# Half-height second product in the scores of the dilated attention

## The chip, the cores and the metric

The program runs on one NeuronCore of a Trainium2 chip. The metric is the device time of one execution in microseconds (us); of several executions the median counts. TensorE (PE in the profile) multiplies: it first loads a stationary operand of up to 128 rows by 128 columns (a weight load, PEld) and then streams a moving operand through it, one step per output column. The rows are the SBUF partitions over which a product sums. VectorE is DVE, ScalarE is ACT, GpSimd is POOL, SyncE is SP.

## The reference

Two transformer blocks stand one after the other, for 512 tokens of width 1024. The second one is a gated feed-forward layer, a mixing layer and another gated feed-forward layer. The change lies in the mixing layer's attention: twelve heads of width 64 in three groups of four, where group 0 looks back 128 tokens, group 1 looks back 512 tokens in steps of 4 and group 2 looks back 2048 in steps of 16. For every head

```
s = einsum('brnqhd,brnkhd->brnhqk', qb, kk) * (Dh ** -0.5)
s = where(allowed, s, -inf);  p = exp(s - max(s))
o = einsum('brnhqk,brnkhd->brnqhd', p, vv) / sum(p)
```

and the three groups' outputs are mixed by a softmax over their log denominators, which for head j is one softmax over the keys of all three groups together.

## The kernel before

Five programs, one for each engine, are written out in order; semaphore waits tie them together, and nothing is reordered by a scheduler. All matrix products work in parts: an operand x is split into a high part rounded to the type fp32r and a low part, the rest, and a product becomes high times high, low times high and high times low.

For the scores, a head has width 64 and the array has 128 rows, and the kernel uses this: `DQ` holds for a head (`key = 2 * g + e_half`) the high part of the queries in the head's own 64 rows and the low part in the other 64 rows. `DKH` holds the high part of the keys in both halves. One product over 128 rows of `DQ` with `DKH` is then (high + low) of the queries times high of the keys. `DKL` holds the low part of the keys in the head's own 64 rows only; the other 64 rows hold zeros, so that a second product over all 128 rows adds high of the queries times low of the keys.

The zeros are written by GpSimd in `pool_dilated` (six copies, one for each of the three groups and two halves), after its last piece of the normalised input and before it multiplies by the rotary cosines. TensorE waits for them (`misc_pool`, "zeros") in `pe_d_scores`.

`pe_d_scores(s)` is called for 16 steps s: j = s // 4 is the head in its group, i = s % 4 the block of 128 queries. It covers up to ten blocks of 128 keys, laid side by side in three PSUM banks (`SALL`), in runs of adjacent blocks of one group; each run is one pair of matmuls of one width. For i = 0 there are 3 runs (width 128 each), for i = 1 3 runs (256), for i = 2 4 runs (256, 256, 128, 384), for i = 3 5 runs (256): 60 runs in all over the 16 steps, 40 of width 256, 16 of 128 and 4 of 384.

There is one set of the three banks. So scores(s+1) wait until DVE has taken the masked maximum of scores(s) (`dve_d_max`, instructions of L86, which also move the scores to SBUF). ACT then takes the exponential, DVE divides by the sum (`dve_d_soft`, L79), TensorE transposes the result (`pe_d_turn`, L69, 128 wide), ACT and DVE copy it back, and TensorE multiplies it with the values (`pe_d_values`, stationary operand of 128 rows by 64 columns, shown as 128*64). On TensorE the loop over s is: scores(s+3), transposes(s), values(s-1). Scores 0 and 1 stand between parts of the projection v2, scores 2 before the loop. At s = 5 the projections of queries and keys for the second half of the heads are put in; then TensorE runs steps 5 to 12 without another large part. After values(7), DVE and ACT also write out the first half's result (`act_d_out`, `dve_d_out`). On DVE the loop is: maximum(s+3), copy(s), division(s+1).

Of the kernel before, what the change touches and what calls it, by code (L numbers as in the profile page):

```python
# [4 lines left out]
S = 512  # L5
# [141 lines left out]
def bass_two_blocks(nc, A, out):  # L147
    ctx = ExitStack()
    with ctx:
# [10 lines left out]
        def sb(shape, dt, offset):  # L160
            names[0] += 1
            return nc.alloc_sbuf_tensor_at(f"t{names[0]}", shape, dt, offset=offset)
# [43 lines left out]
        ZERO = RS[:, 9:10]  # L206
# [56 lines left out]
        DKL = sb([128, 6, S], F32R, AR + 24 * KB)  # L263
# [181 lines left out]
        def count(name):  # L445
            counts.append(Count(name))
            return counts[-1]
# [11 lines left out]
        hmul, h_hi, h_lo, h_lo_pool = count("h_scaled"), count("h_hi"), count("h_lo"), count("h_lo_pool")  # L459
# [8 lines left out]
        misc, misc_act, misc_pool = count("small_dve"), count("small_act"), count("small_pool")  # L468
# [501 lines left out]
        def pool_rotate(e, g, hf, cosv):  # L970
            tm = TMP[ta["rot", g, hf]][:, COLS[hf]]
            e.wait_ge(acc, ("rot", g, hf))
            e.tensor_tensor(tm, tm, cosv[:, COLS[hf]], ALU.mult).then_inc(by_cos, (g, hf))
# [12 lines left out]
        def rows_of(e_half):  # L986
            return slice(64 * e_half, 64 * e_half + 64), slice(64 - 64 * e_half, 128 - 64 * e_half)
# [1191 lines left out]
        def pool_glu_norm(e, nm):  # L2179
            pool_normed(e, nm, 0, UPPER)  # L2180
            pool_normed(e, nm, 1, ALL)
# [8 lines left out]
        def blocks(i):  # L2190
            out_ = [(0, kb) for kb in ((i - 1, i) if i else (0,))]
            return out_ + [(1, kb) for kb in range(i + 1)] + [(2, kb) for kb in range(i + 1)]
# [70 lines left out]
        def pe_d_scores(e, s):  # L2263
            j, i = s // 4, s % 4
            a, e_half = j // 2, j % 2
            runs = []
            for c, (g, kb) in enumerate(blocks(i)):
                if runs and runs[-1][1] == g and c % 4:
                    runs[-1][3] += 1
                else:  # L2270
                    runs.append([c, g, kb, 1])
            for b in range(3):
                banks.take(("ds", s, b), (maxes, ("dx", s)), at=b)
                e.wait_for(banks.free(("ds", s, b)))
            for c, g, kb, n in runs:
                key = 2 * g + e_half
                e.wait_ge(part_lo, ("dq", a, key))
                e.wait_ge(part_hi, (("dk", a, key), 1))
                e.wait_ge(part_lo, (("dk", a, key), 0))
                e.wait_ge(misc_pool, "zeros")  # L2280
                q, kh, kl = DQ[:, key, :], DKH[:, key, :], DKL[:, key, :]
                qs, ks = slice(128 * i, 128 * i + 128), slice(128 * kb, 128 * (kb + n))
                o = SALL[:, 128 * c:128 * (c + n)]
                e.matmul(o, q[:, qs], kh[:, ks], start=True, stop=False)
                t = e.matmul(o, q[:, qs], kl[:, ks], start=False, stop=True)
            t.then_inc(acc, ("ds", s))

        def dve_d_max(e, s):
# [128 lines left out]
        def pool_pz_pool(e, n):  # L2417
            tm = PZ_TMP[n]
            e.wait_ge(misc, ("window", n))
            e.wait_ge(cnt_in, "all")  # L2420
            e.wait_ge(acc, ("dv", 14 if n < 2 else 15))
            e.tensor_tensor(tm[:, :], PZ[:, (n + 1) % 2, 16:16 + S], CNT[:, n, :], ALU.mult).then_inc(
                misc_pool, ("mean", n))
            e.wait_ge(misc_pool, ("mean", n))
            e.tensor_tensor(tm[:, :], tm[:, :], PZC[n][:, :], ALU.subtract).then_inc(misc_pool, ("pool", n))
# [57 lines left out]
        def pe_dilated(e):  # L2483
# [5 lines left out]
            banks.only(3, 4, 5, 6, 7)  # L2489
            pe_linear(e, "v2", WX["v2"], [(0, 256)] * 4, h_tokens(n_mix), lambda n, hf: (v_done, ("dv2", n)), swap=True,  # L2490
                      mid={(F, 0, 0): lambda: pe_rotate(e, pending, F, rot), (F, 0, 2): lambda: pe_d_scores(e, 0),
                           (F, 0, 3): lambda: pe_d_scores(e, 1)})
            pe_d_scores(e, 2)
            for s in range(16):
                if s == 5:
# [170 lines left out]
        def pool_dilated(e):  # L2666
            pool_glu_norm(e, n_mix)
            e.wait_ge(acc, ((("w2", 1, 2), 1), 3, 1))
            e.dma_start(DCOS[:, :], A["k_dcos"]).then_inc(dil_in, by=16)
            e.dma_start(DSIN[:, :], A["k_dsin"]).then_inc(dil_in, by=16)  # L2670
            e.dma_start(rot, A["k_drot"]).then_inc(dil_in, by=16)
            e.dma_start(DM[:, :, :], A["k_dil"]).then_inc(dil_in, "all", by=16)
            e.wait_ge(h_lo_pool, ("mix", 7, 1))
            for s in range(6):
                _, other = rows_of(s % 2)
                if s:
                    e.wait_ge(misc_pool, ("zero", s - 1))
                e.tensor_copy(DKL[other, s, :], ZERO[other, :].to_broadcast([64, S])).then_inc(
                    misc_pool, ("zero", s), "zeros")
            e.wait_ge(misc_pool, "zeros")  # L2680
            e.wait_ge(dil_in, "all")
            for a in range(2):
                for kind in ("dk", "dq"):
                    for n in range(3):
                        pool_rotate(e, (kind, a, n), F, DCOS)
            e.wait_ge(acc, ("ds", 15))
            e.dma_start(CNT[:, :, :], A["k_cnt"].to_broadcast([128, 4, S])).then_inc(cnt_in, "all", by=16)
            for n in range(4):
                pool_pz_pool(e, n)
# [118 lines left out]
        def pool_program(e):  # L2808
            pool_begin(e)
            pool_mla_in(e)  # L2810
            pool_mla(e)
            pool_swa(e)
            pool_ff1(e)
            pool_glu_norm(e, n_glu1)
            pool_normed(e, n_mix, 0, LOWER)
            pool_dilated(e)
            pool_normed(e, n_glu2, 0, LOWER)
            pool_glu_norm(e, n_glu2)
# [109 lines left out]
```

## Time and profile before

| | us |
|---|---|
| median of 3 runs | 2362.05 |
| lowest and highest | 2361.86, 2365.67 |
| profiled execution, its own time | 2361.86 |
| its span in the trace | 2360.1 |
| PE busy | 2247.7 (95%) |
| mean granted TensorE clock | 0.979 of full speed |

The span goes from the first to the last instruction of the trace; the profiled execution's time is 1.8 us longer than it. TensorE is granted either full speed (2.4 GHz, shown as 1.0) or half (1.2 GHz, shown as 0.5). A busy share of PE is a sum of modelled durations that overlap, so the distance from one start to the next says more of a matmul's cost than its duration.

### The profile page before, as it was taken

To read this page: it belongs to the slowest core of one execution; us is meant where nothing else is said; L and a number is where in the kernel's file an instruction comes from. 1 tells how busy PE (TensorE), PEld (TensorE's weight loads), DVE (VectorE), ACT (ScalarE), POOL (GpSimd) and SP (SyncE) were. 2 spreads that over 40 slices of the span, in tenths; PEclk is the share of its full clock that TensorE was granted. 3 is DMA by queue.
4 is the path that set the end of the run, shared out by engine and by line. 5 is a ranking of instruction groups with operands and counts; after the bars stand their busy time and mean duration, and the time that the engine had idled before them with its cause. 6 is when DMAs were issued, how large, how long until landed. Compare 5 with 4: busy or idle time off the path is not lost.

```text
span 2360.1 us, 27745 instructions
## 1 busy us (share of the span) xinstructions
PE 2247.7 (95%) x11491; PEld 1898.9 (80%) x11491; DVE 1224.5 (52%) x1905; ACT 837.3 (35%) x1259; POOL 161.9 (7%) x131
## 2 busy tenths in 40 slices
PE   6897999999988999999989999999899999999999
PEld 3875888888887798888888888887777889888887
DVE  5568666766766764443444433345664535333334
ACT  3555243223245644232233222224443333322222
POOL 7100000000013100000020000002012000000000
PEclk8998999999999999999999999999999999999999
DMA  6224435555521123232313223223112332333320
GB/s 237 78 70 143 143 113 191 196 190 184 203 72 37 37 70 109 89 108 89 100 47 121 89 92 104 82 88 103 53 50 72 99 107 72 107 97 99 94 85 36
DMA packets 143907, 245.43 MB, mean 104 GB/s; under 512 B 4572, under 2 KB 69431, under 8 KB 143655
## 3 DMA queue, kind: packets, MB, share of 16 engines
q1 hardware_dynamic: 142480, 240.60, 30.8%
q0 software_dynamic: 640, 2.70, 0.3%
q8 instruction: 91, 1.49, 0.2%
q10 hardware_dynamic: 662, 0.37, 0.1%
q14 instruction: 34, 0.27, 0.0%
HBM read 241.56 MB, written 2.10 MB: 103 GB/s over the span
## 4 chain that ended last, share of the span: by engine, by line
PE 84%; DVE 9%; ACT 4%; issue 2%; DMA 1%; POOL 1%; SPq 0%; DVEq 0%; ACTq 0%; POOLq 0%
PE PS L66 83%; ACT t L72 4%; DVE t L75 3%; DVE t L83 3%; DVE t L86 1%; PE PS L69 1%; DMA t<-in_w_ada_dram 1%; DVE t L79 1%; POOL t L75 1%; DVE PS L75 0%; DVE t L92 0%; DVE t L80 0%; DVE t L89 0%; DVE t L95 0%; SPq L101 0%
## 5 line engine op out<-in xcount | busy, mean ns | idle before, releaser
L66 PE MATMUL PS<-t,t 128*128 128x512 f32 (+5 forms) x11124 | 2196.7, 360 | 76.5 <-DVE t L75 23.9
L66 PEld LDWEIGHTS PS<-t,t 128*128 128x128 f32 (+2 forms) x11124 | 1853.1, 189 | 416.8 <-issue 74.5
L72 ACT ACTIVATE t<-t 128x512 fp32r<-128x512 f32 (+8 forms) x569 | 539.1, 964 | 1185.1 <-PE PS L66 659.4
L75 DVE TENSOR_TENSOR t<-t,t 128x2048 fp32r<-128x2048 f32 (+9 forms) x506 | 599.2, 1192 | 679.8 <-ACT t L72 677.4
L72 ACT ACTIVATE t<-PS 128x512 f32<-128x512 f32 (+5 forms) x307 | 162.4, 546 | 173.7 <-PE PS L66 129.0
L75 POOL TENSOR_TENSOR t<-t,t 128x512 f32<-128x512 f32 (+2 forms) x71 | 82.1, 1157 | 1227.0 <-ACT t L72 971.3
L72 ACT ACTIVATE t<-t,t 128x256 fp32r<-128x256 f32 (+5 forms) x212 | 112.4, 538 | 106.1 <-DVE t L83 46.3
L83 DVE SCALAR_TENSOR_TENSOR t<-t,t,t 128x1024 f32<-128x1024 f32 (+2 forms) x149 | 140.1, 944 | 9.6 <-ACT t L72 4.1
L83 DVE SCALAR_TENSOR_TENSOR t<-PS,t,t 128x512 f32<-128x512 f32 (+3 forms) x120 | 76.8, 643 | 97.1 <-PE PS L66 81.6
L75 DVE TENSOR_TENSOR t<-t,PS 128x512 f32<-128x512 f32 (+1 forms) x82 | 53.0, 654 | 103.9 <-PE PS L66 98.8
L69 PE MATMUL PS<-t,t 128*128 128x128 f32 (+1 forms) x367 | 59.3, 307 | 32.0 <-DVE t L79 16.9
L69 PEld LDWEIGHTS PS<-t,t 128*128 128x128 f32 (+1 forms) x367 | 47.3, 157 | 40.1 <-issue 25.1
L83 DVE SCALAR_TENSOR_TENSOR t<-t,t,PS 128x256 f32<-128x256 f32 (+1 forms) x133 | 61.9, 488 | 22.3 <-PE PS L66 15.2
L83 DVE SCALAR_TENSOR_TENSOR t<-PS,t 128x512 f32<-128x512 f32 (+1 forms) x68 | 40.3, 596 | 58.8 <-PE PS L66 58.4
L75 DVE TENSOR_TENSOR t<-t 128x512 f32<-128x512 f32 (+3 forms) x99 | 58.1, 587 | 21.9 <-ACT t L72 21.2
L79 DVE TENSOR_SCALAR t<-t,t 128x128 f32<-128x128 f32 (+5 forms) x159 | 57.9, 434 | 5.6 <-DMA t<-in_w_ada_dram 2.6
L79 POOL TENSOR_SCALAR t<-t 128x512 f32<-128x512 f32 x28 | 45.4, 1621 | 62.0 <-DVE t L86 60.7
L86 DVE CUSTOM_DVE_ANT_0 t<-PS,t 128x128 f32<-128x128 f32 (+1 forms) x112 | 35.9, 356 | 21.4 <-PE PS L66 21.3
L75 DVE TENSOR_TENSOR t<-PS,t 128x512 fp32r<-128x512 f32 (+2 forms) x40 | 25.0, 634 | 32.1 <-ACT t L72 20.7
L75 DVE TENSOR_TENSOR PS<-PS,t 128x512 f32<-128x512 f32 (+1 forms) x40 | 27.2, 681 | 20.1 <-PE PS L66 20.0
L72 ACT ACTIVATE t<-PS,t 128x2 f32<-128x2 f32 (+3 forms) x44 | 19.0, 431 | 39.6 <-PE PS L66 39.1
L101 POOL DMA_DIRECT2D t<-in_k_dist_dram x1 | 0.8, 788 | 462.7 <-PE PS L66 462.7
(29 smaller groups left out, 171.4 us busy)
## 6 DMA issues: line engine op xcount, KB each, us to landing
t<-in_w_ff_dram SPq DMA_DIRECT2D x64, 1024.0 KB, 5.3
t<-in_ffn_w_dram SPq DMA_DIRECT2D x60, 1024.0 KB, 5.3
t<-in_w_ada_dram SPq DMA_DIRECT2D x48, 1024.0 KB, 5.5
t<-in_w_in_dram SPq DMA_DIRECT2D x13, 1024.0 KB, 5.2
t<-in_swa_w_qkv_dram SPq DMA_DIRECT2D x6, 1024.0 KB, 5.0
t<-in_ffn_w_dram SPq DMA_DIRECT2D x8, 768.0 KB, 4.4
t<-in_w_in_dram SPq DMA_DIRECT2D x24, 256.0 KB, 3.6
t<-in_mla_w_o_dram SPq DMA_DIRECT2D x4, 1024.0 KB, 6.8
```

The costliest lines, as they stand in the source:

```text
L66: return Instr(self.real and self.real.matmul(o, lhs, rhs, start=start, stop=stop, **more))
L69: return Instr(self.real and self.real.transpose(o, src, ident))
L72: return Instr(self.real and self.real.activation(o, src, func, **more))
L75: return Instr(self.real and self.real.tensor_tensor(o, a, b, op))
L79: return Instr(self.real and self.real.tensor_scalar(o, a, s1, s2, op0))
L83: return Instr(self.real and self.real.scalar_tensor_tensor(o, a, s, b, op0, op1))
L86: return Instr(self.real and self.real.tensor_tensor_reduce(**more))
L101: return Instr(self.real and self.real.dma_start(o, src))
```

## The change

The second matmul of every run reads only the head's own 64 rows of `DQ` and `DKL` instead of all 128. The zeros in the other 64 rows of `DKL` are then read by nobody: GpSimd's six copies, its waits around them and TensorE's wait for them go.

```diff
         def pe_d_scores(e, s):
             j, i = s // 4, s % 4
             a, e_half = j // 2, j % 2
+            own = slice(64 * e_half, 64 * e_half + 64)
...
                 e.wait_ge(part_lo, (("dk", a, key), 0))
-                e.wait_ge(misc_pool, "zeros")
                 q, kh, kl = DQ[:, key, :], DKH[:, key, :], DKL[:, key, :]
                 qs, ks = slice(128 * i, 128 * i + 128), slice(128 * kb, 128 * (kb + n))
                 o = SALL[:, 128 * c:128 * (c + n)]
                 e.matmul(o, q[:, qs], kh[:, ks], start=True, stop=False)
-                t = e.matmul(o, q[:, qs], kl[:, ks], start=False, stop=True)
+                t = e.matmul(o, q[own, qs], kl[own, ks], start=False, stop=True)
             t.then_inc(acc, ("ds", s))
...
             e.dma_start(DM[:, :, :], A["k_dil"]).then_inc(dil_in, "all", by=16)
-            e.wait_ge(h_lo_pool, ("mix", 7, 1))
-            for s in range(6):
-                _, other = rows_of(s % 2)
-                if s:
-                    e.wait_ge(misc_pool, ("zero", s - 1))
-                e.tensor_copy(DKL[other, s, :], ZERO[other, :].to_broadcast([64, S])).then_inc(
-                    misc_pool, ("zero", s), "zeros")
-            e.wait_ge(misc_pool, "zeros")
             e.wait_ge(dil_in, "all")
```

TensorE's instructions stay in the same order and number; only the rows that 60 of them read differ. On GpSimd, between the loads of the constants (`k_drot`, `k_dil`) and the first multiplications by the cosine, the order of the program differs in this way (the rows end in the partitions and columns of the tile; `t_146` is `DKL`, `t_153` is the cosine table):

```order
@@ -79,5 +79,4 @@
 L101 DMA t_75<-in_k_drot_dram 128x128
 L101 DMA t_148<-in_k_dil_dram 128x1280
-L92 CAST t_146<-t_83 64x512 x6
 L75 TENSOR_TENSOR t_61<-t_61,t_153 128x512
 L75 TENSOR_TENSOR t_62<-t_62,t_153 128x512
```

The six copies are gone, and the multiplication by the cosine is what follows the loads.

## Rows read from the trace of the kernel before

**Rows 1.** The page: busy time of each engine, and the chain by engine.

```profile
PE 2247.7 (95%) x11491; PEld 1898.9 (80%) x11491; DVE 1224.5 (52%) x1905; ACT 837.3 (35%) x1259; POOL 161.9 (7%) x131
...
PE 84%; DVE 9%; ACT 4%; issue 2%; DMA 1%; POOL 1%; SPq 0%; DVEq 0%; ACTq 0%; POOLq 0%
```

**Rows 2.** Order of time, POOL, around the zeros: start, length, instruction, [idle before <-releaser].

```profile
1613.15 4.02 POOL L92 CAST t<-t 64x512 fp32r<-64x512 f32 x6
1634.90 1.29 POOL L75 TENSOR_TENSOR t<-t,t 128x512 f32<-128x512 f32 x1 [17.72 <-PE PS L66]
```

**Rows 3.** Groups of PE by shape, whole span: rows*columns of weights, output, count | busy, mean ns.

```profile
L66 PE MATMUL PS<-t,t 128*64 128x128 f32 x440 | 55.4, 280 | 0.0
...
L66 PE MATMUL PS<-t,t 1*128 1x1 f32 x16 | 1.9, 244 | 0.8 <-ACT t L72 0.8
```

**Rows 4.** Order of time, PE, 1690 to 1700 us; a row keeps its first shape.

```profile
1693.25 3.34 PE L66 MATMUL PS<-t,t 128*64 128x128 f32 x26
1696.43 0.49 PE L69 MATMUL PS<-t,t 128*128 128x128 f32 x3
1696.85 3.52 PE L66 MATMUL PS<-t,t 128*64 128x128 f32 x24
```

**Rows 5.** Order of time, PE, short windows from 1691.5 to 1696.8 us.

```profile
1691.43 0.33 PE L66 MATMUL PS<-t,t 128*128 128x128 f32 x2
...
1693.41 1.36 PE L66 MATMUL PS<-t,t 128*64 128x128 f32 x11
...
1695.14 0.39 PE L66 MATMUL PS<-t,t 128*128 128x256 f32 x1
...
1695.37 1.23 PE L66 MATMUL PS<-t,t 128*128 128x256 f32 x9
```

**Rows 6.** Order of time, weight loads, 1690 to 1700 us.

```profile
1693.25 1.72 PEld L66 LDWEIGHTS PS<-t,t 128*64 128x64 f32 x16 [0.17 <-issue]
1695.14 1.25 PEld L66 LDWEIGHTS PS<-t,t 128*128 128x128 f32 x10 [0.17 <-issue]
1696.33 0.35 PEld L69 LDWEIGHTS PS<-t,t 128*128 128x128 f32 x3
```

**Rows 7.** Order of time, weight loads, 44.5 to 46.9 us, where 1-row weights end.

```profile
44.97 1.86 PEld L66 LDWEIGHTS PS<-t,t 1*128 1x128 f32 x16 [1.67 <-issue]
...
46.84 0.19 PEld L66 LDWEIGHTS PS<-t,t 128*128 128x128 f32 x1
```

**Rows 8.** Order of time, PE, scores and transposes of step 8 and after, with idle time.

```profile
1753.30 0.86 PE L66 MATMUL PS<-t,t 128*128 128x128 f32 x6 [0.73 <-issue]
1753.99 0.84 PE L69 MATMUL PS<-t,t 128*128 128x128 f32 x6
...
1756.83 1.06 PE L69 MATMUL PS<-t,t 128*128 128x128 f32 x8 [0.29 <-DVE t L79]
...
1770.95 0.98 PE L66 MATMUL PS<-t,t 128*128 128x256 f32 x6 [1.05 <-DVE t L86]
1772.42 0.30 PE L69 MATMUL PS<-t,t 128*128 128x128 f32 x1 [0.49 <-DVE t L79]
```

**Rows 9.** Order of time, PE, 1668.9 to 1683.5 us, with idle time.

```profile
1669.83 4.08 PE L66 MATMUL PS<-t,t 128*128 128x128 f32 x32 [0.42 <-DVE t L75]
...
1678.64 2.50 PE L66 MATMUL PS<-t,t 128*128 128x256 f32 x10 [1.85 <-DVE t L86]
```

**Rows 10.** Order of time, all engines, 1767 to 1771.2 us: writing out the first half.

```profile
1768.27 0.84 PE L69 MATMUL PS<-t,t 128*128 128x128 f32 x6
...
1769.21 0.69 DVE L75 TENSOR_TENSOR t<-PS,t 128x512 fp32r<-128x512 f32 x1 [1.28 <-ACT t L72]
1769.82 0.28 DVE L86 CUSTOM_DVE_ANT_0 t<-PS,t 128x128 f32<-128x128 f32 x1
```

**Rows 11.** Stretches: length, busy (x) by engine PE to POOL, PEclk, DMA share, GB/s.

```profile
1677.51:1684.30 6.79, 4.18 (x18) 3.79 (x19) 4.49 (x16) 2.61 (x4) 0.00 (x0) 0.50 0.00 0
1753.30:1783.10 29.80, 27.96 (x222) 24.81 (x222) 22.35 (x79) 13.38 (x26) 0.60 (x1) 1.00 0.04 14
```

## The prediction

> **What bounds the kernel now.** I read the page first, then the order of time of the stretch in which the scores stand, PE and its weight loads apart, and last the waits there. PE is busy 95% of the span and carries 84% of the chain that ended last [rows 1]: whatever lengthens PE's own row of work lengthens the program, unless a wait stands right behind it. The scores lie in two stretches, 1668.8 to 1700 us (steps 0 to 7) and 1753.3 to 1783.1 us (steps 8 to 15). In the second, PE shows 27.96 us of busy time in 29.80 at full clock [rows 11], so PE paces the loop there too.
>
> **The part on GpSimd.** The six copies take 4.02 us and end at 1617.17; GpSimd's next work starts at 1634.90, after 17.72 us of idleness that PE ends [rows 2]. Without the copies it waits 4 us longer for the same product. TensorE first needs the zeros at step 0, near 1668.8, 51 us later. This part gives 0. Its cover is these 17.7 us, and it only grows. DVE's and ACT's work is untouched, the DMAs are the same four before and after.
>
> **The part on TensorE.** 60 matmuls read 64 rows instead of 128. Their number and their columns stay, and a matmul is paced by columns, so by itself nothing gets shorter. The question is what it costs to go from weights of one height to weights of another, which now happens twice in each run (full, half, full, half ...), 120 times in all. The trace before has no 64-row matmul; its odd shapes are 440 matmuls of 64 columns and 16 of one row [rows 3], so I take the price from changes of width.
>
> - In the loop, transposes and values alternate between 128*128 and 128*64. Inside a group of 64-column matmuls the starts are 0.109 us apart ((1.36 - 0.27) / 10) [rows 5]. Three transposes at 1696.43 reach the next group, at 1696.85, in 0.42 us [rows 4]: 3 x 0.109 and 0.09 more. The queue of weight loads, which else runs ahead of the matmuls, stands still for 0.17 us before the first load of the new width, and shows no such stop where the scores of 1695.14 go over to the transposes of 1696.33, both 128*128 [rows 6]. So at a change the next weights are not loaded ahead; they wait until the array is empty: 0.09 us.
> - The load itself is then bare. The first score matmul after values starts at 1695.14 and the second at 1695.37, 0.22 to 0.23 us, while the nine from 1695.37 to 1696.43 take 1.06, or 0.118 each [rows 4, 5]: 0.105 more for weights of 128 columns. For 64 columns it is half of that: 16 matmuls take 1.89 us from 1693.25 to 1695.14, which is 16 x 0.109 + 0.15, and 0.09 of the 0.15 is the next change.
> - One change of height exists. 16 loads of 1-row weights last from 44.97 to 46.83; less the last load's own 0.19 that is 1.67 for 15 steps, 0.111 each. The last of them starts at 46.64 and the first 128-row load at 46.84, 0.20 later [rows 7]: again 0.09 above its step. It had a semaphore of its own to pass, so this is a hint, not proof.
>
> A change of height with 128 columns of weights therefore costs 0.09 + 0.105 = 0.195 us, and a run costs 0.39 more. The first entry into a group of scores, from the 64-column values, is paid already; the last exit, to the transposes, is new, so that there are exactly two new changes for each run. For the 40 runs of width 256: 40 x 0.39 = 15.6 us. For width 128, six matmuls take 0.69 us from 1753.30 to 1753.99 [rows 8], 0.115 each, which is the time of a load, while two such matmuls can start 0.05 us apart (0.33 us for two against 0.27 for one) [rows 5]: their streams are shorter than their loads. If the array is empty 0.05 us earlier, a run costs 0.29; if not, 0.39; I take 0.34, in the middle: 16 x 0.34 = 5.4. The four runs of width 384 have the same ends, 4 x 0.35 = 1.4. Together 22.4 us on PE.
>
> The bounds of this price. Above: no row speaks for a change dearer than 0.195 at full clock, but at half clock (the 0.50 of 1677.51 to 1684.30 [rows 11]) everything is slower. Below: if the array is emptied but the loads of half height are hidden, 120 x 0.09 = 10.8 us; if a change of height is no change, 0; below nothing, if a 64-row matmul is let in beside the full one and its load (0.105) vanishes from the path, at most 60 x 0.105 = -6.3. I take the 22.4, since width changes are the nearest rows by far (440 matmuls of that shape), and keep the ends for the range.
>
> The Trainium skill states the rule directly: "Changing tiling mode (not just tile) drains the TensorE" (TensorEngine Tiling (Array Packing), Key Properties), with 64-row tiles as a mode of their own. By that rule, the trace agrees: 0.09 us without a load at each change of width. Against it stands the Trainium skill's page TensorE: Matmul & The Clock Gate, its closing table in the section Why this matters for your kernels ("K=32 single mm = same time as K=128"): by that sentence the sum would be 0, which is rival A.
>
> **What of it is hidden.** PE's idle time before scores(s+1) is no cover: it ends with DVE's maximum of scores(s) (1678.64) [rows 9], and this starts after scores(s) and shifts with them. Cover is only a wait that has another start. There are four. Step 0 stops for 0.42 us in its third run for DVE's rotation of the keys (1669.83) [rows 9], which the two runs before it now fill. Before the transposes of 1756.83 and 1772.42, PE waits 0.29 and 0.49 us for a division that follows the step before, while the longer scores(9) and scores(13) run [rows 8]. And scores(13), at 1770.95, wait 1.05 us [rows 8] for a maximum that DVE could start only at 1769.82, after it had written out the first half's result, which ACT held back 1.28 us; scores(12) had ended near 1768.3 [rows 10], and 3 x 0.34 = 1.0 more brings them to 1769.3, still ahead of DVE. Sum: 0.42 + 0.29 + 0.49 + 1.05 = 2.25 us. The waits in the projections between the stretches hang on PE's own matmuls there and move along.
>
> 22.4 - 2.25 = 20.2 us. Added to the profiled execution, 2361.86, it gives 2382.1; the median of the runs stands 0.2 above that execution, so **2382.3 us, 0.85% slower**.
>
> **The rivals.**
>
> A. A change of height is no change of the array's state: TensorE goes on loading ahead. For it: the new shape keeps all 128 columns, and every priced row but one is a change of columns. Against it: the 1-row case. Price 0, and with the GpSimd part hidden the time stays at 2362, the other side of my forecast. It decides if the load queue shows no stop at 64-row loads.
>
> B. The array is emptied but half of the price is hidden, by the loads of the half height or in one direction only (full to half, since the half weights lie in rows that the full product leaves first). 60 x 0.195 = 11.7 or 120 x 0.09 = 10.8, less 2.25: about 2371.
>
> C. The clock. PE was at half clock after the idle times before 1678.64 [rows 9, 11]; the emptied array now stops for a part of every run in both stretches. If the second stretch ran half of its 108 values and 54 transposes (162 x 0.109 = 17.7 us) at half clock, that would be 9 us more, and the first stretch a few us more: about 2394. Against it: the second stretch stood at 1.00 through waits of 1 us.
>
> D. The 64-row product slips in beside its neighbour: down to 2356. I see no row for it, as its neighbours fill the whole array.
>
> **How the numbers follow.** Forecast 0.62, C 0.13, B 0.12, A 0.09, D 0.04. The median can tell 0.2% (4.7 us, 2357.3 to 2366.8) from no change. Slower holds the forecast, C and B, 0.87; same holds A and a part of D, 0.10; faster 0.03. The range leaves out A and D (0.13) and the far end of C: 2367 to 2398.
>
> **What would show it.** In the trace after, a row of 64*128 matmuls x60, and the load queue of PE standing still about 0.17 us before each of them and before each full one behind it; scores of ten matmuls, 1.29 us from start to transposes before (1695.14 to 1696.43 [rows 4, 5]), near 3.2; the four waits named above gone; GpSimd idle for 21 to 22 us before its first product by the cosine. The forecast is wrong if the 64-row loads follow with no stop (A), if only one side of each pair shows it (B), or if the granted clock falls below 1.00 in the second stretch (C).

## The result and the profile after

The changed kernel takes 2395.8 us in the median (2391.7 to 2396.6, 4 runs) against 2361.95 before. The ratio rests on more executions (the 21 on record of the changed kernel have a median of 2393.4 us): it is 1.0131 with a 95% interval from 1.0118 to 1.0143, so 28 to 34 us slower, 31 in the middle. The profiled execution took 2394.96 us with a span of 2393.1. The page of after, in the lines that answer to [rows 1], and its clock line:

```profile
PE 2283.4 (95%) x11491; PEld 1916.0 (80%) x11491; DVE 1227.0 (51%) x1905; ACT 836.6 (35%) x1259; POOL 156.4 (7%) x125
...
PEclk8998999999999999999999999999789999999999
...
PE 83%; DVE 8%; ACT 3%; issue 3%; POOL 1%; DMA 1%; SPq 0%; DVEq 0%; ACTq 0%; POOLq 0%
```

TensorE executes as many instructions as before and is busy 36 us longer; the other engines' work is unchanged, but for the six copies on POOL. Its clock line has two marks, 7 and 8, in the place of the scores. Where the 33.0 us of span lie is read from three stretches with the same edges in both traces: scores of steps 0 to 7, projections, steps 8 to 15. The columns are those of [rows 11]. Before:

```profile
1668.85:1699.18 30.33, 25.00 (x170) 22.10 (x169) 20.12 (x73) 13.93 (x27) 0.00 (x0) 0.83 0.10 32
1699.18:1753.30 54.12, 51.08 (x205) 39.31 (x205) 28.57 (x30) 25.57 (x33) 9.34 (x6) 0.97 0.23 73
1753.30:1783.14 29.84, 28.00 (x222) 24.81 (x222) 22.39 (x79) 13.42 (x26) 0.60 (x1) 1.00 0.04 14
```

After:

```profile
1668.84:1715.21 46.37, 41.66 (x171) 29.70 (x169) 20.59 (x73) 15.71 (x29) 0.00 (x0) 0.71 0.06 21
1715.21:1769.00 53.79, 49.53 (x205) 38.17 (x205) 29.90 (x29) 23.62 (x31) 8.32 (x6) 1.00 0.23 74
1769.00:1814.63 45.63, 45.57 (x222) 33.98 (x222) 23.16 (x80) 15.27 (x28) 0.59 (x1) 0.81 0.06 22
```

The first stretch starts at the same time in both (1668.84 and 1668.85). The two stretches of scores are longer by 16.04 and 15.79 us, together 31.8; what lies between them is shorter by 0.3 and what comes after is 1.5 longer. Both stretches of scores grew by half, and their mean clock fell from 0.83 to 0.71 and from 1.00 to 0.81.

The weight loads of step 7 (five runs of width 256, at full clock in both) show the mechanism. Order of time, weight loads, after, as in [rows 6]:

```profile
1707.61 3.00 PEld L66 LDWEIGHTS PS<-t,t 128*128 128x128 f32 x10 [0.17 <-issue]
1710.74 0.31 PEld L69 LDWEIGHTS PS<-t,t 128*128 128x128 f32 x3
```

Ten loads and the entry to the transposes take 3.13 us from start to start (1707.61 to 1710.74), where it was 1.19 (1695.14 to 1696.33) [rows 6]. At half clock, in step 3, the loads no longer merge into one row:

```profile
1683.01 0.29 PEld L66 LDWEIGHTS PS<-t,t 64*128 64x128 f32 x1 [0.23 <-issue]
1683.52 0.29 PEld L66 LDWEIGHTS PS<-t,t 128*128 128x128 f32 x1 [0.22 <-issue]
1684.03 0.29 PEld L66 LDWEIGHTS PS<-t,t 64*128 64x128 f32 x1 [0.22 <-issue]
```

Each load, of either height, stands 0.51 us behind the last, with 0.22 us in which the load queue waits for nothing that the profile shows.

On GpSimd the copies of [rows 2] are gone, and the next product waits longer and starts where it did, at 1634.88 (1634.90 before):

```profile
1634.88 1.29 POOL L75 TENSOR_TENSOR t<-t,t 128x512 f32<-128x512 f32 x1 [21.80 <-PE PS L66]
```

### The profile page after: what moved, and what is told of

Same layout as the page of the kernel before. It is cut to its first block, busy times and chain, and to the rows that moved or that the text cites. A ratio compares the mean times of both kernels' runs of the same rounds, so it can differ in the third digit from the quotient of the medians.

```text
span 2393.1 us, 27739 instructions
## 1 busy us (share of the span) xinstructions
PE 2283.4 (95%) x11491; PEld 1916.0 (80%) x11491; DVE 1227.0 (51%) x1905; ACT 836.6 (35%) x1259; POOL 156.4 (7%) x125
## 4 chain that ended last, share of the span: by engine, by line
PE 83%; DVE 8%; ACT 3%; issue 3%; POOL 1%; DMA 1%; SPq 0%; DVEq 0%; ACTq 0%; POOLq 0%
PE PS L66 82%; ACT t L72 3%; DVE t L83 3%; DVE t L75 2%; DVE t L86 1%; PE PS L69 1%; POOL t L79 1%; DMA t<-in_w_ada_dram 1%; DVE t L79 1%; POOL t L75 1%; DVE t L80 0%; DVE PS L75 0%; DVE t L92 0%; DVE t L89 0%; DVE t L95 0%
## 5 line engine op out<-in xcount | busy, mean ns | idle before, releaser
L66 PE MATMUL PS<-t,t 128*128 128x512 f32 (+5 forms) x11124 | 2228.3, 362 | 74.5 <-DVE t L75 22.8
```

Source lines behind the costliest of these rows:

```text
L66: return Instr(self.real and self.real.matmul(o, lhs, rhs, start=start, stop=stop, **more))
```

## The experiments

All ratios are against the kernel before on the same chip. Each edit is shown against the changed kernel, or, for the two runs on the kernel before and the one in the other attention, against that; lines left out are marked by dots.

### The part on GpSimd alone

```diff
             for c, g, kb, n in runs:
...
+                e.wait_ge(misc_pool, "zeros")
...
+            for s in range(6):
+                _, other = rows_of(s % 2)
...
+                e.tensor_copy(DKL[other, s, :], ZERO[other, :].to_broadcast([64, S])).then_inc(
+                    misc_pool, ("zero", s), "zeros")
...
```

> The changed kernel with GpSimd's six copies of zeros, its waits and TensorE's wait for them put back. Theory (all of the loss is in the changes of weight height on TensorE): as the changed kernel, 2395.8 us within 3, because GpSimd has 17 us of idle time behind the copies. Rival P (the removed copies moved something else on GpSimd or on the shared memory port): a time clearly apart from 2395.8.

Measured: 2393.7 us, 1.0132 (1.0116 to 1.0147), against 1.0131 for the change. Both stretches have the clock (0.71 and 0.81) of the changed kernel, and the copies stand where they stood before, with 17.73 us of idle time behind them. The GpSimd part does nothing that these runs can tell; rival P falls.

### How many changes of height: 18, 32, 72, 120

Mirrored (72 changes):

```diff
-            for c, g, kb, n in runs:
+            for r, (c, g, kb, n) in enumerate(runs):
...
-                e.matmul(o, q[:, qs], kh[:, ks], start=True, stop=False)
-                t = e.matmul(o, q[own, qs], kl[own, ks], start=False, stop=True)
+                pair = [(q[:, qs], kh[:, ks]), (q[own, qs], kl[own, ks])]
+                for m, (lhs, rhs) in enumerate(pair[::-1] if r % 2 else pair):
+                    t = e.matmul(o, lhs, rhs, start=m == 0, stop=m == 1)
```

> The changed kernel, with every second run of a step in the order half, full, so that two half products or two full ones stand side by side: 72 changes of height where the changed kernel has 120. Theory: at full clock 72 x 0.145 to 0.195 = 10 to 14 us over the kernel before, less 2 hidden, and with some 3 to 8 us for the half clock 2374 to 2383; two half-height matmuls in a row 0.12 us apart at full clock. Rival H (a half-height matmul is slow wherever it stands): 2396 as the changed kernel, with 60 half-height matmuls as before.

Both products of half height, without the queries' low part times the keys' high part (18 changes; the 19 of the expectation count one too many, since step 3 follows step 2 at the same height):

```diff
-                e.matmul(o, q[:, qs], kh[:, ks], start=True, stop=False)
+                e.matmul(o, q[own, qs], kh[own, ks], start=True, stop=False)
```

> Both products of every run read the head's own 64 rows; the product of the queries' low part with the keys' high part is left out. 120 half-height matmuls, but only one new change of height in each of 16 steps (the exit to the transposes; the entry from 64-column weights was paid already, but for steps 0 to 2, which come from full weights: 19 in all). Theory: 19 x 0.145 to 0.195 = 3 to 4 us less about 1 hidden, so 2364 to 2366, and half-height matmuls 0.118 us apart within a step. Rival H: twice the loss of the changed kernel or about it, 2395 to 2430.

All full products of a step first, then its half ones (32 changes); only the first product in a PSUM bank starts a sum there, and the others write into columns that it has cleared:

```diff
+            later, bank_ = [], None
             for c, g, kb, n in runs:
...
-                e.matmul(o, q[:, qs], kh[:, ks], start=True, stop=False)
-                t = e.matmul(o, q[own, qs], kl[own, ks], start=False, stop=True)
+                e.matmul(o, q[:, qs], kh[:, ks], start=c // 4 != bank_, stop=False)
+                bank_ = c // 4
+                later.append((bank_, o, q[own, qs], kl[own, ks]))
+            for m, (bank_, o, lhs, rhs) in enumerate(later):
+                t = e.matmul(o, lhs, rhs, start=False, stop=m + 1 == len(later) or later[m + 1][0] != bank_)
```

> The changed kernel, with all full products of a step first and then all its half ones: 32 changes of height where the changed kernel has 120. Theory: 32 x 0.145 to 0.195 = 5 to 6 us, less 1 to 2 hidden and 1 to 4 us for the clock: 2366 to 2371. Rival H (the half-height matmul is what costs): 2395.

| kernel | changes | ratio (interval) | median us | changes in step 7 | step 7, us |
|---|---|---|---|---|---|
| before | 0 | 1 | 2361.95 to 2362.5 | 0 | 1.19 |
| all half | 18 | 1.0010 (1.0000 to 1.0019) | 2365.0 | 1 | 1.38 |
| grouped | 32 | 1.0026 (1.0017 to 1.0036) | 2369.5 | 2 | 1.56 |
| mirrored | 72 | 1.0072 (1.0055 to 1.0089) | 2379.6 | 6 | 2.35 |
| changed | 120 | 1.0131 (1.0118 to 1.0143) | 2395.8 | 10 | 3.13 |

The last column is from the first weight load of step 7 to the first one of its transposes, all at full clock: all half, grouped and mirrored in this order:

```profile
1695.62 1.25 PEld L66 LDWEIGHTS PS<-t,t 64*128 64x128 f32 x10 [0.17 <-issue]
1697.00 0.31 PEld L69 LDWEIGHTS PS<-t,t 128*128 128x128 f32 x3
```

```profile
1700.96 1.43 PEld L66 LDWEIGHTS PS<-t,t 128*128 128x128 f32 x10 [0.17 <-issue]
1702.52 0.31 PEld L69 LDWEIGHTS PS<-t,t 128*128 128x128 f32 x3
```

```profile
1703.69 2.21 PEld L66 LDWEIGHTS PS<-t,t 128*128 128x128 f32 x10 [0.17 <-issue]
1706.04 0.31 PEld L69 LDWEIGHTS PS<-t,t 128*128 128x128 f32 x3
```

Above 1.19 these are 0.19, 0.37, 1.16 and 1.94 us for 1, 2, 6 and 10 changes: 0.19 for each, whatever the order. The one change of all half goes from half to full height, and grouped adds one from full to half, so each direction has this price. Ten half-height loads in a row are as close as ten full ones (1.25 us for ten in both: here and in [rows 6]), so a half-height matmul costs no more than a full one; rival H falls. The medians of all half, mirrored and grouped lie in the ranges expected for them. The whole program loses more for each change the more of them there are: by the ratios 2.4, 6, 17 and 31 us, or 0.13, 0.19, 0.24 and 0.26 us for each. So there is something beside the 0.19; the section on the clock has it.

### The same edit in another place

```diff
+            own = slice(64 * (h % 2), 64 * (h % 2) + 64)
...
-                t = e.matmul(o, QS[:, h, qs], KL[:, g, ks], start=False, stop=True)
+                t = e.matmul(o, QS[own, h, qs], KL[own, g, ks], start=False, stop=True)
```

> The kernel before, with the half-height second product in the other attention's scores (64 pairs of width 256 in pe_s_scores; the low part of the queries times the low part of the keys is left out). Theory: 128 new changes of height at 0.195 us, 25 us on TensorE at full clock, less what idle times of that stage cover (at most some 9 us there: 2.9, 1.9, 2.9 and 1.1 us), so 2378 to 2395; half-height matmuls 0.31 us before the next one. Rival (the price is special to the place, four full and half matmuls between DVE's maxima): under 10 us, 2372 or less.

Measured: 2375.0 us, 1.0049 (1.0035 to 1.0063), some 12 us: less than the theory's range (16 to 33 us) and more than the rival's (under 10), so neither forecast held. Eight loads at full clock, of one head of the kernel before and one of this:

```profile
756.30 1.01 PEld L66 LDWEIGHTS PS<-t,t 128*128 128x128 f32 x8 [0.17 <-issue]
757.26 0.79 PEld L69 LDWEIGHTS PS<-t,t 128*128 128x128 f32 x7
```

```profile
778.03 2.37 PEld L66 LDWEIGHTS PS<-t,t 128*128 128x128 f32 x8 [0.17 <-DVE t L86]
780.53 0.53 PEld L69 LDWEIGHTS PS<-t,t 128*128 128x128 f32 x5
```

2.50 us against 0.96: 1.54 for 8 changes, again 0.19. The price is the same in this other place. My sum was too high for two reasons, which the stage from 717 us to the end of its heads shows, in the kernel before and in this one:

```profile
717.00:814.46 97.46, 86.53 (x601) 75.50 (x601) 73.16 (x263) 62.67 (x191) 21.21 (x14) 0.98 0.14 44
```

```profile
717.00:827.66 110.66, 109.79 (x604) 83.85 (x604) 75.50 (x265) 63.44 (x191) 21.06 (x14) 0.97 0.12 39
```

TensorE had stood idle for 10.9 of 97.5 us, and for 0.9 now. It is busy for 23 us more, where I had expected 25, and 10 us of these went into waits, where I had expected at most 9. The stage is 13.2 us longer.

### The clock

Full products of width 512 that nobody reads, on a free PSUM bank, fill TensorE's waits:

```diff
+        def pe_fill(e, at, count):
...
+            for _ in range(count):
+                t = e.matmul(PS[:, b, :], HHI[:, 0, 0:128], HHI[:, 1, :], start=True, stop=True)
...
+            pe_fill(e, 2, 6)
             pe_d_scores(e, 2)
...
+                if s in (0, 1):
+                    pe_fill(e, s + 3, {0: 7, 1: 5}[s])
                 if s < 13:
                     pe_d_scores(e, s + 3)
```

> The changed kernel with 6, 7 and 5 full matmuls of width 512, whose result nobody reads, put on TensorE ahead of scores 2, 3 and 4, where it waits 1.58, 1.85 and 1.28 us for the maximum. Theory C1 (the granted clock falls to half because of these waits): the clock stays at 1.00 from 1677 to 1701, and the time falls by 5 to 6 us to 2390. Theory C2 (it falls because every second weight load now finds the array empty): the clock of that stretch still has 0.5 in it for most of the time, and the time stays at 2395 to 2397.

Measured: 2383.5 us, 1.0090 (1.0075 to 1.0105): by the two ratios 10 us less than the changed kernel, where C1 gave 5 to 6. Its two stretches:

```profile
1669.19:1706.63 37.44, 37.40 (x188) 27.02 (x186) 20.17 (x73) 14.19 (x27) 0.00 (x0) 0.95 0.08 26
1760.77:1805.04 44.27, 44.27 (x222) 33.48 (x222) 23.18 (x80) 15.42 (x28) 0.59 (x1) 0.85 0.06 24
```

With the waits filled, the first stretch stands at 0.95 instead of 0.71 and is 8.9 us shorter, though it does 18 matmuls more. What C1 said of the clock comes out there, and what C2 said (0.5 for most of the stretch) does not. The waits are not the whole cause all the same: they are as long in the kernel before (1.58, 1.85 and 1.47 us, at 0.83) as in the changed one (1.58, 1.85 and 1.28 us, at 0.71). A filler ends a wait and adds dense work as well, so this run does not give each its share.

The second stretch has no filler and is 1.4 us shorter than in the changed kernel. Just ahead of it the two differ in one wait: TensorE waits 0.73 us for scores 8, as in the kernel before, and 1.97 us in the changed kernel. Order of time, the filled kernel and then the changed one:

```profile
1760.77 0.81 PE L66 MATMUL PS<-t,t 128*128 128x128 f32 x3 [0.73 <-issue]
```

```profile
1767.82 1.09 ACT L72 ACTIVATE t<-PS 128x512 f32<-128x512 f32 x2
1769.00 0.70 PE L66 MATMUL PS<-t,t 128*128 128x128 f32 x2 [1.97 <-issue]
```

The profile names nothing that this wait hangs on, but the scores start 0.09 us after the end of ACT's last copy in both the kernel before and the changed one. How long it is follows the clock of the projections ahead of it. In the kernel before, all half, grouped, filled and before filled they show 0.97 and the wait is 0.73 us; in the changed one, mirrored and zeros kept they show 1.00, and it is 1.97. There TensorE is done with the projections earlier against ACT and only waits longer. The stretch of the projections gains 0.3 us.

> The changed kernel filled ahead of scores 2, 3 and 4 as in e4, and with 4 more such matmuls ahead of scores 8, where TensorE waited 0.73 us (1.97 in the changed kernel). If that wait brings the half clock of the second stretch (6.83 + 3.41 + 3.41 us in e4): it goes, and the time falls by 2 to 4 us to 2380. If the changes of height bring it: still 7 us or more at half clock there, and the time stays within 1 us of e4's 2383.5.

Against the changed kernel filled:

```diff
-                if s in (0, 1):
-                    pe_fill(e, s + 3, {0: 7, 1: 5}[s])
+                if s in (0, 1, 5):
+                    pe_fill(e, s + 3, {0: 7, 1: 5, 5: 4}[s])
```

Measured: 2380.4 us, 1.0071 (1.0057 to 1.0085), 3 us below the last in the median. Its second stretch:

```profile
1759.82:1801.03 41.21, 41.21 (x224) 31.07 (x223) 23.09 (x80) 15.27 (x28) 0.59 (x1) 0.92 0.06 22
```

TensorE waits neither ahead of it nor inside, and the mean clock is 0.92: the expectation for the wait comes out in the time, and yet clock is lost where no wait is left.

> The kernel before, with the same 6, 7 and 5 matmuls that nobody reads ahead of scores 2, 3 and 4. Theory: its 10.24 us at half clock from 1677.5 go, and with them some 35 starts 0.213 us apart instead of about 0.115: 3 us less, 2359.5; the clock row of that stretch at 1.00 or near it. Rival (the clock does not hang on these waits): no change, 2362.5.

The same fillers in the kernel before: 2359.5 us, 0.9985 (0.9976 to 0.9995), 3 us faster, as expected. Its two stretches, the first against 30.33 us at 0.83 before:

```profile
1670.51:1698.14 27.63, 26.02 (x188) 22.45 (x186) 20.02 (x73) 14.00 (x27) 0.00 (x0) 1.00 0.11 36
1752.31:1782.14 29.83, 28.00 (x222) 24.80 (x222) 22.38 (x79) 13.43 (x26) 0.60 (x1) 1.00 0.04 13
```

This run and the changed kernel filled differ in the rows that the second products read, and in the copies of zeros that e1 found to cost nothing. The second stretch has the same 0.73 us ahead of it in both, and stands at 1.00 here and at 0.85 there. So the changes of height bring half clock by themselves, with TensorE busy all the time. Steps 8 to 15 in these kernels:

| kernel | changes of height | wait ahead, us | mean clock | length, us |
|---|---|---|---|---|
| before | 0 | 0.73 | 1.00 | 29.84 |
| before, filled | 0 | 0.73 | 1.00 | 29.83 |
| all half | 8 | 0.73 | 1.00 | 30.25 |
| grouped | 16 | 0.73 | 1.00 | 31.22 |
| mirrored | 36 | 1.97 | 0.87 | 38.69 |
| changed | 60 | 1.97 | 0.81 | 45.63 |
| changed, filled | 60 | 0.73 | 0.85 | 44.27 |
| changed, filled more | 60 | 0 | 0.92 | 41.21 |

With up to 16 changes the wait of 0.73 us brings no half clock, with 60 it does, and with 60 and no wait some is left. Both take part, though the fillers that end a wait also add dense work, and no run separates the shares. Each row is one execution; zeros kept repeats the changed kernel, with 0.81 again.

What the clock costs is an estimate from this table. Call the length times what the mean clock lacks to 1 the lost clock. From changed to filled more it falls from 0.19 x 45.63 = 8.7 us to 0.08 x 41.21 = 3.3 us, and TensorE's list in the stretch is the same (the four fillers end where it starts). So 5.4 us of lost clock cost 4.4 us, 0.82 for each; from changed to filled it is 0.67, from filled to filled more 0.92. With none lost the stretch would take about 41.21 - 3.3 x 0.82 = 38.5 us, 8.7 more than before (8.3 to 9.2 with the other two).

> The kernel before with the filling of e5 (6, 7 and 4), and besides 14, 18 and 12 matmuls of width 512 of ones, which nobody reads, at the start of the other attention, at the start of the first gated layer and ahead of the pooling product, where TensorE waited 3.33, 4.69 and 3.03 us. Theory (a wait brings half clock behind it, and filling it keeps the clock): four or so of the 3.41 us stretches at half clock go (684, 1227 and 1237, 1831 us), each worth up to 1.7 us: 2353 to 2357. Rival (the short half clock stretches cost nothing, because something else ends last there): 2359.5 as e5.

```diff
         def pe_swa(e):
+            pe_keep(e, "swa", 14)
...
         def pe_glu(e, i, nm, nxt):
+            if i == 1:
+                pe_keep(e, "glu", 18)
...
         def pe_pool_out(e):
+            pe_keep(e, "pool", 12)
```

The fillers ahead of scores 2, 3 and 4 stay in, with 6, 7 and 4 matmuls. Measured: 2360.6 us, 0.9998 (0.9989 to 1.0007): nothing gained over the kernel before. The profile says in part why; order of time, PE, at the other attention, the first gated layer and the pooling product:

```profile
685.30 14.09 PE L66 MATMUL PS<-t,t 128*128 128x256 f32 x84 [3.24 <-DVE t L83]
...
1224.83 8.56 PE L66 MATMUL PS<-t,t 128*128 128x256 f32 x68
1238.03 2.26 PE L66 MATMUL PS<-t,t 128*128 128x256 f32 x9 [4.64 <-issue]
...
1829.36 1.85 PE L66 MATMUL PS<-t,t 128*128 128x512 f32 x7 [0.45 <-DVE t L75]
```

The first two fillings were put ahead of matmuls that were ready or nearly so, and the long waits (3.24 and 4.64 us, 3.33 and 4.69 before) still stood behind these. The third one filled its wait (0.45 us left of 3.03), and the mean clock from 1826 to 1850 us rose from 0.93 to 1.00; what that was worth cannot be told from the total. So the run says little of the theory, and the kernel before with 6, 7 and 5 fillers has the lowest ratio found.

## Why the prediction was right, and what it missed

**The sign and the cost of a change: right.** The price grows with the number of changes, one and ten alike at 0.19 us, and is the same in either direction; where the rows show single loads (step 3), the load queue stops before each. That it could be read from changes of width in the trace before was a guess from 440 matmuls of another shape; the runs showed the two to be the same. Rival A (no change of state), rival B (one direction or the loads hidden) and rival D (the half product slips in) fall with the column of step 7.

**0.195 us for a change with 128 columns of weights: right**, 0.19 measured in four kernels and in another stage.

**Width 128, for which I took 0.34 between 0.29 and 0.39: the lower end.** Six matmuls up to the first of the transposes took 0.69 us before (1753.30 to 1753.99) [rows 8]. In step 12 of the changed kernel, at full clock, they take 1.53 us, 0.84 for six changes, 0.14 each:

```profile
1793.87 1.46 PEld L66 LDWEIGHTS PS<-t,t 128*128 128x128 f32 x6 [0.17 <-issue]
1795.40 0.31 PEld L69 LDWEIGHTS PS<-t,t 128*128 128x128 f32 x3
```

That is 0.05 less than with width 256, what an array that is empty 0.05 us earlier would give, as the row of two matmuls in [rows 5] had hinted. It takes 1.0 us off the sum (16 x 0.06).

**What is hidden: right for the second stretch.** Its waits of 1.05, 0.49 and 0.29 us [rows 8] went, with 0.05 left of them; in the first stretch the 0.42 of [rows 9] went and the wait before scores 4 was 0.19 shorter, while the two others stayed at 1.58 and 1.85, as they must when the maximum shifts along. That the waits in the projections only move along was not so: the one ahead of scores 8 grew from 0.73 to 1.97 us. The end of the projections hung on more than PE's own matmuls.

**The sum, 20.2 us: close for what it counted, but a term was missing.** Each stretch of scores has 20 runs of width 256, 8 of 128 and 2 of 384. By the price above and the cover, the second one should be longer by 20 x 0.39 + 8 x 0.28 + 2 x 0.35 - 1.83 = 8.9 us; without lost clock it would be 8.7 longer by the estimate above. In the changed kernel it is 15.8 longer. The difference, 7 us, is the clock, and the first one is alike.

The step of the prediction that failed is the choice of the likeliest case, in which the clock costs nothing. By the prediction's own sign (the clock of the second stretch falls below 1.00) its forecast of 2382.3 us is wrong: the clock fell to 0.81, and rival C, to which I gave 0.13 and 2394 us, is what happened. The measured 2395.8 lies in my range of 2367 to 2398 only because that range took C in. C's parts were off too: it had 9 us in the second stretch and a few in the first, and the runs show about 7 in each. My argument against it was that the second stretch had stood at 1.00 through waits of 1 us. That holds with no changes of height; with 60 of them the clock was 0.85 behind the same wait ahead and with no idle time inside. The longer wait of 1.97 us added to it, but was not needed.

The two stretches lost 0.29 x 46.4 + 0.19 x 45.6 = 22.1 us of clock against 5.2 before. At 0.82 us each (an estimate, taken over from the second stretch to the first) that is 14 us of the 31.8, and the changes of height are the other 18; with 0.67 and 0.92 it is 11 to 16, and 16 to 20.

## What to carry to other kernels

Slicing a product to half the rows saved TensorE nothing here (ten half-height loads and ten full ones both take 1.25 us), and where it stands between products of full height it costs two changes of height, 0.19 us each with 128 columns of weights, because the load queue stops at each. Pad with zeros instead, or put products of one height side by side; and price such a change by the nearest change of shape that the trace already has. Ask then what the holes do to the clock: here the clock cost an estimated 11 to 16 us beside 16 to 20 for the changes themselves.

## What the runs showed of the hardware

TensorE can be busy by the profile for every microsecond of a stretch and be granted 0.85 or 0.92 of its clock there, when the height of its weights changes 60 times in 41 to 44 us; with no change, the same work stood at 1.00. One wait in the projections, 2.31 us in the kernel before and 2.30 in the changed one, was followed by half clock in the first (0.97 in the stretch) and not in the second (1.00), and the next wait was 0.73 us in the first and 1.97 in the second. And matmuls that nobody reads, in waits of 1.3 to 1.9 us, made the kernel before 3 us faster and the changed one 10 us faster.
